# Start of a transformer block: tiles and weight chunks by turns, seven progressive chunks, angles later, gate dots spread

## What is computed

```python
mod = jax.nn.silu(c) @ w_ada[l] + b_ada[l]
shift, scale, gate = jnp.split(mod, 3, axis=-1)
h = rmsnorm(x, g_pre[l]) * (1.0 + scale[:, None, :]) + shift[:, None, :]
proj = h @ w_in[l]
rq, rk, rv, rg, nq, nkv, ngl, ng = jnp.split(proj, offsets, axis=-1)
...   # retention and sparse attention on the parts, with rotary positions
y = rmsnorm(mixed @ w_out[l], g_post[l])
x = x + gate[:, None, :] * y
```

## Time and profile before

| | |
|---|---|
| median of 3 runs | 1504.77 us |
| lowest and highest | 1500.78 and 1505.94 us |
| span of the profiled execution | 1500.5 us |
| PE busy | 1452.3 us (97%) |
| DVE busy | 828.7 us (55%) |
| ACT busy | 683.7 us (46%) |
| POOL busy | 201.9 us (13%) |
| mean granted TensorE clock | 0.992 |

### The profile page before, as it was taken

How to read it: one execution, slowest core, us unless ns; L and a number is a source line. 1 busy time by engine, 2 the same in 40 slices (tenths; PEclk the granted TensorE clock), 3 DMA queues, 4 the chain that set the end, 5 groups by cost and what they waited for, 6 DMA issues and landing times.

```text
span 1500.5 us, 22048 instructions
## 1 busy us (share of the span) xinstructions
PE 1452.3 (97%) x8524; PEld 1226.9 (82%) x8524; DVE 828.7 (55%) x1455; ACT 683.7 (46%) x1302; POOL 201.9 (13%) x319
## 2 busy tenths in 40 slices
PE   7999999899999999999999999989999999999997
PEld 4887876678988888888998777769988888888996
DVE  6678646776645444432275577574754444422474
ACT  4565536676542222221363556676532232321563
POOL 0000000443310000000130222451300000000221
PEclk9999999999999999999999999999999999999999
DMA  9542440004033333333404211503133333332321
GB/s 365 197 167 85 124 157 10 1 2 169 2 99 98 98 98 98 94 95 94 152 3 167 71 57 43 169 16 99 33 109 98 94 92 96 103 105 92 120 85 56
DMA packets 42148, 146.71 MB, mean 98 GB/s; under 512 B 4673, under 2 KB 7121, under 8 KB 41682
## 3 DMA queue, kind: packets, MB, share of 16 engines
q1 hardware_dynamic: 37986, 128.99, 27.2%
q0 software_dynamic: 3072, 15.71, 2.8%
q10 hardware_dynamic: 1008, 0.89, 0.2%
HBM read 141.39 MB, written 4.19 MB: 97 GB/s over the span
## 4 chain that ended last, share of the span: by engine, by line
PE 84%; DVE 9%; ACT 3%; issue 2%; DMA 1%; POOL 0%; DVEq 0%; SPq 0%; ACTq 0%; POOLq 0%
PE B L285 22%; PE B L287 22%; PE B L286 22%; PE CROW_P L285 3%; PE CROW_P L287 3%; PE CROW_P L286 3%; PE B L1789 2%; PE B L2025 1%; DVE AL L1381 1%; DVE WADA L1143 1%; PE CROW_P L1868 1%; ACT T L622 1%; PE CROW_P L1768 1%; ACT AH L622 1%; DVE WL L1110 1%
## 5 line engine op out<-in xcount | busy, mean ns | idle before, releaser
L285 PE MATMUL B<-UH,WH 128*128 128x512 f32 (+1 forms) x1008 | 374.7, 372 | 4.6 <-DVE WL L1110 3.7
L287 PE MATMUL B<-UH,WL 128*128 128x512 f32 (+1 forms) x1008 | 372.3, 369 | 0.0
L286 PE MATMUL B<-UL,WH 128*128 128x512 f32 (+1 forms) x1008 | 372.3, 369 | 0.0
L622 ACT ACTIVATE WH<-RAW 128x1024 fp32r<-128x1024 f32 x174 | 182.6, 1052 | 120.0 <-DMA RAW<-in_stream 111.6
L285 PEld LDWEIGHTS B<-UH,WH 128*128 128x128 f32 x1008 | 190.4, 189 | 38.0 <-issue 5.0
L286 PEld LDWEIGHTS B<-UL,WH 128*128 128x128 f32 x1008 | 190.3, 189 | 32.0
L287 PEld LDWEIGHTS B<-UH,WL 128*128 128x128 f32 x1008 | 190.2, 189 | 32.0
L1110 DVE TENSOR_TENSOR WL<-RAW,WH 128x1024 fp32r<-128x1024 f32 x94 | 116.0, 1240 | 143.8 <-ACT WH L622 143.7
L1462 DVE TENSOR_TENSOR WL<-RAW,WH 128x1024 fp32r<-128x1024 f32 x80 | 98.0, 1226 | 76.7 <-ACT WH L622 73.9
L622 ACT ACTIVATE T<-B 128x256 f32<-128x256 f32 (+5 forms) x186 | 86.5, 465 | 109.9 <-PE B L287 63.3
L622 ACT ACTIVATE T<-T 128x512 f32<-128x512 f32 (+3 forms) x131 | 68.7, 525 | 130.8 <-DVE T L1466 119.2
(11 more groups left out here) (419 smaller groups left out, 3146.2 us busy)
## 6 DMA issues: line engine op xcount, KB each, us to landing
RAW<-in_stream SPq DMA_DIRECT2D x202, 512.0 KB, 3.7
WADA<-in_w_ada SPq DMA_DIRECT2D x8, 1024.0 KB, 16.7
RAW<-in_stream SPq DMA_DIRECT2D x16, 384.0 KB, 3.5
WADA<-in_w_ada SPq DMA_DIRECT2D x2, 2048.0 KB, 11.5
W<-in_w POOLq DMA_DIRECT2D x2, 2048.0 KB, 12.1
X<-in_x SPq DMA_DIRECT2D x2, 1024.0 KB, 11.0
DECAY<-in_decay POOLq DMA_DIRECT2D x1, 2048.0 KB, 9.6
X<-in_x POOLq DMA_DIRECT2D x2, 1024.0 KB, 8.2
```

What stands on the lines that cost most here:

```text
L285: nc.tensor.matmul(out, lh, rh, start=start, stop=False, **kw)
L286: nc.tensor.matmul(out, lh, rl, start=False, stop=False, **kw)
L287: return nc.tensor.matmul(out, ll, rh, start=False, stop=stop, **kw)
L622: return nc.scalar.activation(out, in_, func, **kw)
```

## The change

The first product takes seven progressive chunks. Its order is by turns: with each new tile n the chunks before n, then with chunk n all tiles so far. On DVE each late tile is now dots, scaling, UL and then the weight part. The squares have a buffer each; DVE adds squares 4 and 5, and 6 and 7, and PE sums six instead of eight tiles. ACT copies the row silu(c) from PSUM to `CROW`, from which the dots read, since the bank is now used by the seventh chunk; POOL copies it again to `CROW_X` for the gate dots. The first angles stand behind the last tile and weight part 7, before the masks; the second in iteration 6, with their sines in 9 and the table in 11. The gate dots are in iterations 10, 12, 16, 22, 24 and 25, their rows loaded in three parts, and `DECAY` is fetched behind the last of them. The padding matmuls are 12, 8 and 16 instead of 24 and 12, at other places.

```diff
@@ -55,11 +55,11 @@
...
 ADA = 24
-ADA_GATES = ((16, 4), (20, 4))
-FIRST = 6
-FIRST_STEPS = ([(0, 0), (1, 0), (0, 1), (1, 1)] + [(k, 2) for k in range(2)] + [(2, d) for d in range(3)]
-               + [(k, 3) for k in range(3)] + [(3, d) for d in range(4)] + [(k, 4) for k in range(4)] + [(4, d) for d in range(5)]
-               + [(k, 5) for k in range(5)] + [(k, d) for k in range(5, 8) for d in range(6)])
+ADA_GATES = ((16, 4), (20, 1), (21, 3))
+GATE_DOTS = {10: (16, 17), 12: (17, 18), 16: (18, 21), 22: (21, 22), 24: (22, 23), 25: (23, 24)}
+FIRST = 7
+FIRST_STEPS = ([(0, 0), (1, 0), (0, 1), (1, 1)] + [s for n in range(2, 6) for s in [(n, d) for d in range(n)] + [(k, n) for k in range(n + 1)]]
+               + [(k, 6) for k in range(6)] + [(k, d) for k in range(6, 8) for d in range(7)])
 SLOTS = 4
...
@@ -97,7 +97,8 @@
...
         HL = hb("HL", 44, [P, FT, SEQ], F32R)
-        WADA = hb("WADA", 0, [P, ADA, DM])
+        WADA = hb("WADA", 0, [P, 2 * KT, DM])
+        WADA_X, CROW_X = at("WADA_X", OFF_X + 8 * KB, [P, DM]), at("CROW_X", OFF_X + 12 * KB, [P, DM])
         QRH, QRL = hb("QRH", 0, [P, 4, SEQ], F32R), hb("QRL", 8, [P, 4, SEQ], F32R)
...
@@ -160,7 +161,7 @@
...
         POSI = at("POSI", OFF_T + 11 * 2 * KB, [P, SEQ], I32)
-        SQ = at("SQ", OFF_U + 16 * KB, [P, 4, SEQ])
+        SQ = at("SQ", OFF_U + 16 * KB, [P, KT, SEQ])
         CROW = at("CROW", OFF_T + 4 * 2 * KB, [P, DM])
...
@@ -288,7 +289,7 @@
         E = {n: Event(n) for n in (
-            "silu_c converted ada_dot gain_cols x_sq angle sines x_stats u_t u_hi u_lo "
+            "crow silu_c converted ada_dot gain_cols x_sq angle sines x_stats u_t u_hi u_lo "
             "y_copy y_sq y_sum y_st y_ln y_rstd y_t x_new nu_hi nu_lo n_sq n_sum n_st n_ln n_rstd half "
...
@@ -300,6 +301,8 @@
         E["x_rstd"] = Event("", E["silu_c"], 1)
+        E["x_pair"], E["clock"] = Event("", E["converted"], 1), Event("", E["x_stats"], KT)
+        masks = Event("", E["converted"], 3)
         pl_y, at_x, at_m, at_hi, at_lo = (Event(n) for n in "pl_y at_x at_m at_hi at_lo".split())
...
@@ -440,22 +443,29 @@
...
                 m, many = ADA_GATES[n]
-                sp.dma_start(WADA[:, m:m + many, :],
-                             a["w_ada"][m * P:(m + many) * P].rearrange("(m p) k -> p m k", p=P)).then_inc(pair_here[n], 16)
+                source = a["w_ada"][m * P:(m + many) * P]
+                if n == 1:
+                    wait(sp, E["u_lo"], KT)
+                    sp.dma_start(WADA_X[:, :], source).then_inc(pair_here[n], 16)
+                    return
+                wait(sp, E["ada_dot"], 16 + 2 * n)
+                sp.dma_start(WADA[:, 12:12 + many, :], source.rearrange("(m p) k -> p m k", p=P)).then_inc(pair_here[n], 16)
             sp.dma_start(CROW[0:1, :], a["c"]).then_inc(c_here, 16)
...
                              a["x"][4 * k * P:(4 * k + 4) * P].rearrange("(k p) n -> p k n", p=P)).then_inc((x_here, x_rest)[k], 16)
-            for n in range(4):
-                load_pair(n + 1)
+            load_pair(1)
+            for n in range(SLOTS):
                 load(n, n)
-            for k in range(5, KT):
-                load_pair(k)
+                if n > 0:
+                    load_pair(n + 1)
             for d in range(SLOTS, N_DENSE):
-                if d in (10, 11):
-                    load_gates(d - 10)
+                for k in ((), (5,), (), (6, 7))[d - SLOTS] if d < 8 else ():
+                    load_pair(k)
+                if d in (10, 11, 21):
+                    load_gates((10, 11, 21).index(d))
                 if d - SLOTS in PHASE_OF:
...
@@ -476,7 +486,10 @@
...
             fetch(CMASK[:, :, :, :], a["cmask"], tabs_here)
-            wait(pool, E["u_t"], KT)
+            wait(pool, E["crow"], 1)
+            wait(pool, E["u_lo"], KT)
+            E["crow"].mark(nc.gpsimd.tensor_copy(CROW_X[:, :], CROW[:, :]))
+            wait(pool, E["ada_dot"], ADA)
             fetch(DECAY[:, :, :], a["decay"], decay_here)
...
@@ -681,12 +694,11 @@
             def squares(src, k):
-                wait(act, E["x_stats"], k - 1 if k >= 4 else 0)
-                return E["x_sq"].mark(f(SQ[:, k % 4, :], src, ACT.Square))
+                return E["x_sq"].mark(f(SQ[:, k, :], src, ACT.Square))
             def rms(bank, tile):
-                wait(act, E["x_stats"], KT + 2)
+                wait(act, E["x_stats"], KT)
                 E["x_rstd"].mark(f(tile[:, :], bank[:, :], ACT.Ln, scale=1.0 / DM, bias=EPS))
...
@@ -699,6 +711,8 @@
...
             table_set(EXP_LN_SET)
+            wait(act, E["x_stats"], 2)
+            E["crow"].mark(f(CROW[:, :], CROW_P[:, :], ACT.Copy))
             for k in range(KT):
...
@@ -708,20 +722,22 @@
...
                 wait(act, E["u_t"], k + 1)
+                if k == KT - 1:
+                    wait(act, E["clock"], 1)
                 E["u_hi"].mark(f(UH[:, k, :], X[:, k, :], ACT.Identity, bias=MOD[:, k:k + 1]))
...
                 u_high(k)
-                if k < 7:
-                    hi_of_weights(k + 1)
-                if k == 3:
+                for d in ((1,), (2,), (3,), (4,), (5, 6), (7,), (), ())[k]:
+                    hi_of_weights(d)
+                if k == 4:
                     for dst, src in ((CONST[:, 0:2, :], a["const"][:, 0:2, :]), (CONST[:, 3:5, :], a["const"][:, 3:5, :]),
...
                         act.dma_start(dst, src).then_inc(const_here, 16)
-            wait(act, E["converted"], 2)
+            wait(act, masks, 1)
             act.wait_ge(tabs_here, 16 * 3)
             for d in range(32):
-                if FIRST + 2 <= d + 2 < 32:
+                if 8 <= d + 2 < 32:
                     hi_of_weights(d + 2)
...
@@ -733,7 +749,7 @@
...
                     wait(act, E["sines"], 2)
-                if d == 14:
+                if d == 9:
                     wait(act, E["angle"], 2)
...
@@ -748,6 +764,7 @@
...
                 elif kind == GATE:
+                    wait(act, E["ada_dot"], ADA if d >= 28 else 0)
                     E["gates"].mark(f(RG[:, d // 16, d % 4, :], bank[:, :], ACT.Silu))
...
@@ -1140,7 +1157,8 @@
             def dots(m):
-                E["ada_dot"].mark(stt(WADA[:, m, :], WADA[:, m, :], 1.0, (CROW_P if m < 2 * KT else CROW)[:, :], ALU.mult, ALU.mult,
+                row = WADA[:, m, :] if m < 16 else WADA[:, m - 4, :] if m < 20 else WADA_X[:, :] if m == 20 else WADA[:, m - 9, :]
+                E["ada_dot"].mark(stt(row, row, 1.0, (CROW if m < 2 * KT else CROW_X)[:, :], ALU.mult, ALU.mult,
                                       accum_out=DOTS[:, m:m + 1]))
...
@@ -1158,6 +1176,8 @@
...
                 for m in range(first, end):
+                    if m == 20:
+                        dve.wait_ge(pair_here[1], 32)
                     dots(m)
...
@@ -1173,35 +1193,38 @@
...
             dve.wait_ge(vecs_here, 32)
-            wait(dve, E["x_stats"], 2)
+            wait(dve, E["crow"], 1)
             modulation(0)
+            for k in (4, 6):
+                wait(dve, E["x_sq"], k + 2)
+                E["x_pair"].mark(tt(SQ[:, k, :], SQ[:, k, :], SQ[:, k + 1, :], ALU.add))
+            modulation(1)
+            wait(dve, E["x_rstd"], 2)
+            u_scaled(0)
+            lo_of_weights(0)
+            u_low(0)
+            u_scaled(1)
+            u_low(1)
+            lo_of_weights(1)
+            for k in range(2, KT):
+                modulation(k)
+                u_scaled(k)
+                u_low(k)
+                if k < 6:
+                    lo_of_weights(k)
+                if k == 5:
+                    lo_of_weights(6)
+            lo_of_weights(7)
             dve.wait_ge(pos_here, 16 * 2)
...
             reduced(T[8][:, :], T[7][:, :])
-            modulation(1)
-            wait(dve, E["x_rstd"], 2)
-            u_scaled(0)
-            u_scaled(1)
-            lo_of_weights(0)
-            u_low(0)
-            u_low(1)
-            lo_of_weights(1)
-            for k in range(2, KT):
-                modulation(k)
-                u_scaled(k)
-                if k < 6:
-                    lo_of_weights(k)
-                u_low(k)
-            v.tensor_copy(CROW[:, :], CROW_P[:, :])
-            for d in range(6, 8):
-                lo_of_weights(d)
             dve.wait_ge(tabs_here, 16 * 3)
...
             v.tensor_copy(TRI[:, :, :], T[0][:, 0:2 * P].rearrange("p (a n) -> p a n", a=2))
-            E["converted"].mark(v.tensor_copy(MASKB[:, :, :], T[0][:, 2 * P:4 * P].rearrange("p (a n) -> p a n", a=2)))
+            masks.mark(v.tensor_copy(MASKB[:, :, :], T[0][:, 2 * P:4 * P].rearrange("p (a n) -> p a n", a=2)))
             def finish_tables(n):
...
@@ -1221,19 +1244,20 @@
...
                     E["q_rot"].mark(tt(T[10][:, :], T[10][:, :], T[11][:, :], ALU.add))
-                if FIRST + 2 <= d + 2 < 32:
+                if 8 <= d + 2 < 32:
                     lo_of_weights(d + 2)
...
```

(26 more changed lines are left out.)

## The result

The changed kernel takes 1505.36 us (median of 18 runs, 1503.67 to 1507.33), the kernel before 1503.30 us in as many runs; the ratio is 1.0013, 95% interval 1.0007 to 1.0019. It is slower by 2 us, clear of noise and within 0.3%. The profiled execution spans 1502.3 us against 1500.5.

The account below looks back on a forecast made before the run. PE is busy 97% of the span, with the beginning bound by DVE. Chunk 8 +5.3, low clock +1.5 and chunk 18 -4.37 sum to +2.4 us: 1507.2 from a median of 1504.77, range 1501.5 to 1511.0.

Parts of the forecast that it names:

- Dots and chunk 18: Moving the gate dots on DVE removes PE's wait before chunk 18 and its low clock: 4.37 us back.
- R: End of the Exp giving the row factor after the sum of squares; forecast 20.66 instead of 22.38.
- M: Start of DVE's dots for tile 2 in the changed kernel; forecast at 26.81.
- Tiles: On DVE a late tile with its weight part behind UL takes 6.14 us, the 0.79 wait for UH unfilled.
- U: End of the last UL on DVE in the changed kernel; forecast at M + 35.8.
- Chunk 8: PE waits there for weights behind ACT's queue and late masks; start at 80.7 for 75.44, +5.3 us.
- POOL's copy: GpSimd's copy of CROW beside DVE's angle delays the masks by 1.0 us, bounds 0 and 1.22.
- Low clock: After PE's 3.8 us wait at chunk 8 the granted clock is low, costing 1.5 us.
- covered: Rival: no wait at chunk 8 because ACT's queue is done sooner; -3.0 us, 1501.8; chance 0.12.
- much faster: Rival: the beginning itself gains, over 4.5 us faster in all, 1499; chance 0.08.
- the dots that bring nothing: Rival: another operation still holds chunk 18 back; +6.8 us, 1511.5; chance 0.08.
- The low clock over the squares: Rival: PE's clock stays low through the sum of squares, delaying R; +4.1 to +5.8 us, 1510; chance 0.15.

Follow-up runs that it names:

- The dots alone: Kernel before with only the gate dots, second angle, its sines and its table moved to other iterations: 1498.2 us, ratio 0.9968 against the kernel before.
- part 8 early: Changed kernel with ACT making the high part of chunk 8's weights in iteration 5 instead of 6: ratio 0.9980 against the kernel before.
- the two-by-two of masks and chunks: Changed kernel (1.0013) with masks ahead of the angle (1.0009), six progressive chunks instead of seven (1.0011), or both (0.9993); ratios against the kernel before.

## Why the prediction was right

- Dots and chunk 18: 4.37 us to be had. The dots alone gave 4.47. Right, and the 0.28 us of the late chunk 17 belonged to it.
- Squares and M: R was forecast at 20.66, one low stretch of clock included. The profiled execution had none; R is 19.78 and DVE, busy with the dots of tile 1 until 19.92, sets M = 25.92 instead of 26.81. This term was off by 0.9 us, and the Ln came at 18.52 for the 19.4 named as a sign. The expectation that the low stretch returns was a guess from one trace; it comes in some executions only. Where it came, M was on either side of the forecast: 26.42 with POOL's copy late (clock 0.76 in 12 to 18) and 27.36 with part 8 early (0.61). That the adds are done before PE needs them was wrong by a little: PE waits 0.31 us for the first of them.
- Tiles: 6.14 us each, measured 6.14 (25.92 to 32.06); U at M + 35.8, measured M + 35.82. The unfilled wait of 0.79 is there in every tile, in DVE's timeline of the changed kernel, which answers to the earlier trace rows:

```profile
28.71 0.75 DVE L1188 SCALAR_TENSOR_TENSOR X<-X,GS,T 128x512 f32<-128x512 f32 x1
30.25 0.75 DVE L1193 SCALAR_TENSOR_TENSOR UL<-X,MOD,UH 128x512 fp32r<-128x512 f32 x1 [0.79 <-ACT UH L635]
30.92 1.22 DVE L1125 TENSOR_TENSOR KEPT_L<-RAW,KEPT_H 128x1024 fp32r<-128x1024 f32 x1
32.06 1.22 DVE L1161 SCALAR_TENSOR_TENSOR WADA<-WADA,CROW 128x1024 f32<-128x1024 f32 x1
```

- PE to the end of chunk 7: forecast M + 50.04, measured M + 50.26. As M came 0.9 early, chunk 7 ended 0.7 later than before and not 1.4.
- Chunk 8: forecast at M + 53.9 with the copy, measured M + 53.81; a wait of 3.8, measured 3.55. So the forecast of 80.7 for its start was late by the 0.9 of M alone. Both causes named, the masks and the short cover, were needed to explain it, as the two-by-two of masks and chunks showed. I had named the masks as what comes last, by 0.3 us without the copy; with it they come last by 1.03, and 0.84 of that is the copy. Without moving them the number of chunks changes nothing, and moving them alone gives 1.0, since the table load, which waits for the end of the first progressive chunk, then comes last: that is the lost cover.
- POOL's copy: 1.0, measured 0.84. Its own length beside DVE, 1.89 us, was not foreseen; alone it is 1.04, inside the bounds of 0 and 1.22. The rows 10 that the prediction took as agreeing fit roughly: the UL was 0.49 us longer where it overlapped the add by 0.68.
- Low clock: 1.5, measured 1.58.
- Chunks 12, 18 and 27, SP's queue and DECAY: no wait at any of them, as costed.
- Sum: +2.4 on 1500.5, so 1502.9; measured 1502.3. By terms it is +1.5 up to chunk 31; the other 0.3 to 0.4 us lie behind it. There the fourteen traces of this case take from 1299.6 to 1302.2 us, from the last matmul of chunk 31 to the end, in no order of the edits, so these 0.4 us cannot be told from chance. Up to chunk 31, the part that the prediction worked out, the forecast is +2.4 and the measurement +1.4: the 1.0 between them is mostly the M term, and that the spans agree to 0.6 is in part luck.
- Median: 1507.2 for 1505.36. The difference of the medians, 2.06, is near the 2.4; most of the miss is the base, since the three runs shown had a median of 1504.77 and eighteen have 1503.30.
- The rivals: covered and much faster fell with the 3.55 us, and the dots that bring nothing fell with the dots alone. The low clock over the squares did happen, in other executions, at about its price (U at 59.02 for 57.31): of the ten profiles with 12 and 8 padding matmuls four read under 0.8 in 12 to 18 and five 1.00. How often it came in the eighteen timed runs isn't known; their median stayed near the forecast's change.

## What to carry to other kernels

Before an engine's work is taken into a block that runs earlier, count what the block covered: here two whole chunks on PE hid 9 us of work on ACT (a table load, SiLU, sines and evictions), and one does not. A wait that holds a whole in-order queue, such as the one for the masks, should be met by the first thing its maker does, not by the last. When an engine waits for a partner in every round of a loop, keep a piece of independent work in that gap; taking it out to get the result sooner delays all later rounds by the gap.

The gain of a bundle can sit in one line of it. The new places of the dots and of the second angle, a few lines, were worth 4.5 us; the rest of the change cost more than that.

## What the runs showed of the hardware

- GpSimd and DVE slow each other: a copy of 128x1024 took 1.04 us alone and 1.89 beside DVE, and DVE's cast of 128x512 from integers 1.26 instead of 0.42. The Trainium skill (SBUF — State Buffer, Who interferes with whom) has the second to issue block fully. The trace agrees: the copy was issued at 61.89 under DVE's weight part from 61.66 and took 0.85 us more, the cast was issued at 62.79 under the copy and took 0.84 more. With the masks first the copy fell on another cast (to `IDB`, 1.06 us for 0.22).
- The wait for the masks was carried by the SiLU, not by the table load: the load ran at 63.27 with six chunks, 6.3 us ahead of the masks. That hides 1.28 us.
- PE's granted clock over the squares, with the same padding and squares ahead of it, was 0.58 to 1.00 on the mean of 12 to 18 from one profile to the next.
- At chunk 8, waits of PE of 0.75 and 0.96 us left the clock high; the five between 2.38 and 3.39 us were each followed by a low stretch that cost some 1.5 us (chunk 8 to the last matmul of chunk 31 takes 122.5 to 122.7 us there, 121.07 behind the wait of 0.75). The length of the wait alone doesn't settle it: in the changed kernel one of 1.24 us, before 24.92, was followed by 0.50 in 26 to 28, and in the kernel before one of 1.57 us, before 37.42, by 1.00 in 38 to 40.
